# Hybrid attention and RWKV-7 encoder block on one core: two packed transpositions a scan unit instead of four, and rounded products for the head sums, the LoRA's low parts and the attention spreadings

## What is computed

```python
h = rms_norm(x, norm1_w)
z_attn, z_rwkv, z_gate = split(h @ w_in)          # one projection, 12064 columns
q, k = rms_norm(per head of 64) ; o_attn = sum over 3 groups of share * attention(q, k, v)
kk = k_raw * k_k ; kk = kk / sqrt(sum over the head's 64 of kk * kk)
decay = f(decay_w0 + tanh(w_lo) @ decay_w2) ; iclr = sigmoid(iclr_a0 + a_lo @ iclr_a2)
S = S diag(w) + (S (-kk)) (kk*a)^T + v k^T ; y = S r     # per head, forward and backward
x = x + (gates_a * (o_attn @ w_branch_attn) + gates_b * (o_rwkv @ w_branch_rwkv)) @ w_out
x = x + (silu(h2 @ w_gate) * (h2 @ w_up)) @ w_down        # h2 = rms_norm(x, norm2_w)
```

## Time and profile before

| | |
|---|---|
| median of 3 runs | 3433.13 us (3432.88 to 3439.56) |
| the profiled execution, its own time | 3441.14 us |
| its span, first to last instruction | 3439.4 us |
| TensorE busy | 3350.3 us, 97% |
| TensorE's weight loads | 2746.7 us, 80% |
| VectorE busy | 1901.4 us, 55% |
| ScalarE busy | 1233.8 us, 36% |
| GpSimd busy | 1539.0 us, 45% |
| mean granted TensorE clock | 0.991 |
| products L1597 to L1599, projection | 448.0 + 427.2 + 427.4 us |
| products L756 to L758, scan | 189.3 + 170.4 + 170.9 us |
| GpSimd L430 and L433, inversions | 269.8 + 271.0 us |

### The profile page before, as it was taken

How to read it: one execution, slowest core, us unless ns; L and a number is a source line. 1 busy time by engine, 2 the same in 40 slices (tenths; PEclk the granted TensorE clock), 3 DMA queues, 4 the chain that set the end, 5 groups by cost and what they waited for, 6 DMA issues and landing times.

```text
span 3439.4 us, 42457 instructions
## 1 busy us (share of the span) xinstructions
PE 3350.3 (97%) x16199; PEld 2746.7 (80%) x16199; DVE 1901.4 (55%) x2418; ACT 1233.8 (36%) x1963; POOL 1539.0 (45%) x1461
## 2 busy tenths in 40 slices
PE   7999999999998999999899999999999999999998
PEld 6777787777777888888678878888888888888886
DVE  3655465555557877876342022555556456456556
ACT  4433324444234545554343232223233233233232
POOL 4533333333328888888275433322332233223323
PEclk9999999999899999999999999999999999999999
DMA  5444454433354555554543323333332333333323
GB/s 169 133 132 135 123 156 121 120 115 92 87 151 121 126 133 125 129 143 116 191 153 123 123 74 110 92 111 92 104 112 83 117 99 92 110 92 104 111 83 107
DMA packets 666051, 405.08 MB, mean 118 GB/s; under 512 B 193534, under 2 KB 597178, under 8 KB 665338
## 3 DMA queue, kind: packets, MB, share of 16 engines
q1 hardware_dynamic: 665850, 402.38, 40.3%
HBM read 347.05 MB, written 54.53 MB: 117 GB/s over the span
## 4 chain that ended last, share of the span: by engine, by line
PE 49%; DVE 1%; ACT 0%; issue 0%; POOL 0%; DMA 0%; SPq 0%; DVEq 0%; ACTq 0%; POOLq 0%
PE f_bank L2164 9%; PE f_bank L2165 9%; PE f_bank L2166 9%; PE f_bank L2202 4%; PE f_bank L2204 4%; PE f_bank L2203 4%; PE f_bank L2142 2%; PE f_bank L2143 2%; PE f_bank L2144 2%; PE f_bank L2085 1%; PE f_bank L2087 1%; PE f_bank L2086 1%; PE f_bank L2120 0%; DMA orw_plain<-oat 0%; DVE orw_plain L2658 0%
## 5 line engine op out<-in xcount | busy, mean ns | idle before, releaser
L2453 POOL TENSOR_TENSOR w_lo_b<-w_raw_b,w_hi_b 128x1024 fp32r<-128x1024 f32 x176 | 434.1, 2468 | 905.1 <-ACT w_hi_b L2329 903.1
L1285 POOL TENSOR_TENSOR ring_w_rounded<-ring_w_plain,ring_w_hi 128x1024 fp32r<-128x1024 f32 x138 | 333.7, 2419 | 598.9 <-ACT ring_w_hi L1298 598.9
L2164 PE MATMUL f_bank<-act_rounded,w_lo_b 128*128 128x512 f32 x1408 | 549.5, 390 | 1.2 <-DVE act_rounded L2565 1.2
L2165 PE MATMUL f_bank<-act_rounded,w_hi_b 128*128 128x512 f32 x1408 | 548.1, 389 | 0.0
L2166 PE MATMUL f_bank<-act_rounded,w_hi_b 128*128 128x512 f32 x1408 | 548.0, 389 | 0.0
L1597 PE MATMUL slab_ps<-h_hi,ring_w_rounded 128*128 128x512 f32 x1088 | 448.0, 412 | 2.7 <-DVE h_lo L1434 2.4
L1599 PE MATMUL slab_ps<-h_hi,ring_w_hi 128*128 128x512 f32 x1088 | 427.4, 393 | 0.0
L1598 PE MATMUL slab_ps<-h_lo,ring_w_hi 128*128 128x512 f32 x1088 | 427.2, 393 | 0.0
L2329 ACT CAST w_hi_b<-w_raw_b 128x1024 fp32r<-128x1024 f32 x176 | 185.0, 1052 | 448.7 <-DMA w_raw_b<-in_w_ffn_up_dram 202.2
L2164 PEld LDWEIGHTS f_bank<-act_rounded,w_lo_b 128*128 128x128 f32 x1408 | 264.6, 188 | 55.9 <-DVE act_rounded L2565 1.1
L2166 PEld LDWEIGHTS f_bank<-act_rounded,w_hi_b 128*128 128x128 f32 x1408 | 264.6, 188 | 55.3
(11 more groups left out here) (419 smaller groups left out, 6247.5 us busy)
## 6 DMA issues: line engine op xcount, KB each, us to landing
ring_w_plain<-in_w_in_dram SPq DMA_DIRECT2D x190, 512.0 KB, 4.1
w_raw_b<-in_w_ffn_gate_dram SPq DMA_DIRECT2D x88, 512.0 KB, 3.6
w_raw_b<-in_w_ffn_up_dram SPq DMA_DIRECT2D x88, 512.0 KB, 3.6
w_raw_b<-in_w_ffn_down_dram SPq DMA_DIRECT2D x42, 512.0 KB, 4.1
zt<-slab_out SPq DMA_DIRECT2D x65, 256.0 KB, 4.3
...
```

The costliest lines, as they stand in the source:

```text
L1285: pool.tensor_tensor(raw_half(w_lo, h), raw_half(w_raw, h), hi_half(h).bitcast(F32), ALU.subtract).then_inc(lo_ready, 1)
L2164: pe.matmul(o, wl[:, k, :], act_hi[:, kk, :], start=kk == 0, stop=False)
L2165: pe.matmul(o, wh[:, k, :], act_lo[:, kk, :], start=False, stop=False)
L2453: pool.tensor_tensor(low(r), slab_raw(j % 2), high(r).bitcast(F32), ALU.subtract).then_inc(slab_low, 1)
```

## The change

It does four things.
- The scan's `a` and `v` stand side by side in one tile (`av`), as do `b` and `k` (`bk`), 64 columns each: two transpositions of four products take the place of four. Their results lie one above the other; ScalarE copies each head's block to its place (`heads_down`), and v's straight into a `v_t` that GpSimd set to zero before. `b_bd` and `k_bd`, still needed by `ab` and `ak`, are now made by ScalarE (`bd`, the last of its slot) from `bk`. `a_bd` and `v_bd` are gone.
- The head sums are two rounded products. ScalarE makes the squares twice, plain and rounded, and GpSimd the low part, after a half slab's low part. A tile stands after each.
- The low activations of decay and rate have zeros in the other 64 rows, so that both products of a job have 128 rows.
- The spreadings are two rounded products each; VectorE makes high and low part of the shares. Six stand in each of the last two slots, instead of eight and four, and five tiles ahead of the first. Slots without another rule begin with two tiles.

Left out below: the declarations of the new tiles, the counts, and SP's waits with new names.

```diff
@@ scan: orders and shares @@
-PE_SLOT = (("x1", "u"), ("ab", "v"), ("lx", "u"), ("ak", "v"), ("x3", "u"), ("ta", "v"), ("tb", "v"), ("qg", "u"),
-           ("tk", "v"), ("tv", "v"), ("yh", "u"), ("akv", "v"), ("ts", "u"))
-GATE_SHARE = {"ab": 2, "ak": 2, "tb": 3, "tv": 2, "akv": 3, "ts": 4}
+PE_SLOT = (("x1", "u"), ("ab", "v"), ("lx", "u"), ("ak", "v"), ("x3", "u"), ("av", "v"), ("qg", "u"),
+           ("bk", "v"), ("yh", "u"), ("akv", "v"), ("ts", "u"))
+GATE_SHARE = {"ab": 2, "ak": 2, "av": 3, "bk": 3, "akv": 3, "ts": 3}
 DVE_SLOT = (("ab", "v"), ("xadd", "u"), ("ak", "v"), ("decays", "w"), ("qg", "u"), ("operands", "w"), ("state", "u"))
-ACT_SLOT = (("x1", "u"), ("wx", "u"), ("ta", "v"), ("tb", "v"), ("ux", "u"), ("tk", "v"), ("tv", "v"),
-            ("exps", "w"), ("vbd", "w"), ("st", "u"), ("akv", "v"), ("y", "u"))
+ACT_SLOT = (("x1", "u"), ("wx", "u"), ("ux", "u"), ("at", "v"), ("vt", "v"), ("bt", "v"), ("kt", "v"),
+            ("exps", "w"), ("v", "w"), ("st", "u"), ("akv", "v"), ("y", "u"), ("bd", "w"))
@@ phase_scan @@
-for t in (a_bd, b_bd, k_bd, v_bd, ak_bd, w_bd, u_bd, *d_bd):
+for t in (b_bd, k_bd, ak_bd, w_bd, u_bd, *d_bd):
     pool.memset(t[:, :, :], 0.0).then_inc(zeroed, 1)
 for t in low:
+    pool.memset(t[:, :, :], 0.0).then_inc(zeroed, 1)
+for t in v_t:
     pool.memset(t[:, :, :], 0.0).then_inc(zeroed, 1)
 for it in range(NUNIT // 2):
     m = blocks[it % 2]
...
+def heads_down(dst, src):
+    for e in range(2):
+        ins = act.copy(dst[CH * e:CH * e + CH, :, :], src[:, :, CH * e:CH * e + CH])
+    ins.then_inc(taken_act, 1)
@@ phase_scan, ScalarE @@
-elif name == "ta":
-    act.wait_ge(made, PE_AT["ta", n])
-    compact(xar[st][:, :, CH:P], bank[4], taken_act)
-elif name == "tb":
-    act.wait_ge(made, PE_AT["tb", n])
-    compact(rb[st][:, :, CH:P], bank[5], taken_act)
+elif name == "at":
+    act.wait_ge(made, PE_AT["av", n])
+    heads_down(xar[st][:, :, CH:P], bank[4][0:CH, :, :])
+elif name == "vt":
+    if n == 0:
+        act.wait_ge(zeroed, N_ZERO + NSET)
+    for e in range(2):
+        r = slice(CH * e, CH * e + CH)
+        ins = act.copy(v_t[st][r, :, r], bank[4][CH:P, :, r])
+    ins.then_inc(taken_act, 1)
+elif name == "bt":
+    act.wait_ge(made, PE_AT["bk", n])
+    heads_down(rb[st][:, :, CH:P], bank[1][0:CH, :, :])
+elif name == "kt":
+    heads_down(rk[st][:, :, CH:P], bank[1][CH:P, :, :])
...
-elif name == "tk":
-    act.wait_ge(made, PE_AT["tk", n])
-    compact(rk[st][:, :, CH:P], bank[1], taken_act)
-elif name == "tv":
-    act.wait_ge(made, PE_AT["tv", n])
-    act.copy(v_t[st][:, :, :], bank[4][:, :, :]).then_inc(taken_act, 1)
...
-elif name == "vbd":
+elif name == "v":
     act.wait_ge(landed, 96 * (n + 1))
     if n >= 1:
-        act.wait_ge(made, PE_AT["tv", n - 1])
+        act.wait_ge(made, PE_AT["av", n - 1])
+    act.copy(av[:, :, CH:P], ordered(v_in, s)).then_inc(taken_act, 1)
+elif name == "bd":
+    act.wait_ge(taken_dve, DVE_AT["operands", n])
+    if n >= 1:
+        act.wait_ge(made, PE_AT["ak", n - 1])
     for e in range(2):
         r = slice(CH * e, CH * e + CH)
-        ins = act.copy(v_bd[r, :, r], ordered(v_in, s)[r])
+        act.copy(b_bd[r, :, r], bk[r, :, 0:CH])
+    for e in range(2):
+        r = slice(CH * e, CH * e + CH)
+        ins = act.copy(k_bd[r, :, r], bk[r, :, CH:P])
     ins.then_inc(taken_act, 1)
 elif name == "akv":
@@ phase_scan, VectorE @@
 if n >= 1:
-    dve.wait_ge(made, PE_AT["tv", n - 1])
+    dve.wait_ge(made, PE_AT["bk", n - 1])
...
-for e in range(2):
-    r = slice(CH * e, CH * e + CH)
-    dve.tensor_tensor(b_bd[r, :, r], ordered(b0, s)[r], by_scan(e_inv, s)[r], ALU.mult)
-    dve.tensor_tensor(k_bd[r, :, r], ordered(k_in, s)[r], by_scan(e_inv, s)[r], ALU.mult)
+dve.tensor_tensor(bk[:, :, 0:CH], ordered(b0, s), by_scan(e_inv, s), ALU.mult)
+dve.tensor_tensor(bk[:, :, CH:P], ordered(k_in, s), by_scan(e_inv, s), ALU.mult)
 dve.wait_ge(prep_ready, n + 1)
-for e in range(2):
-    r = slice(CH * e, CH * e + CH)
-    ins = dve.tensor_copy(a_bd[r, :, r], t[r, :, CH:P])
-ins.then_inc(taken_dve, 1)
+dve.tensor_copy(av[:, :, 0:CH], t[:, :, CH:P]).then_inc(taken_dve, 1)
@@ phase_scan, TensorE @@
 elif name == "ab":
-    pe.wait_ge(taken_dve, DVE_AT["operands", n])
-    if n >= 1:
-        pe.wait_ge(taken_act, ACT_AT["tk", n - 1])
+    pe.wait_ge(taken_act, ACT_AT["bd", n])
...
-elif name == "ta":
+elif name == "av":
+    pe.wait_ge(taken_act, ACT_AT["v", n])
     if n >= 1:
-        pe.wait_ge(taken_act, ACT_AT["tv", n - 1])
+        pe.wait_ge(taken_act, ACT_AT["vt", n - 1])
     for q in Q:
-        ins = pe.transpose(bank[4][:, q, :], a_bd[:, q, :], g.ident[:, :])
-elif name == "tb":
-    before = [x for x in (n - AHEAD - 1, n - AHEAD - 2) if has_stage("state", x)]
-    if n >= 1:
-        pe.wait_ge(taken_act, ACT_AT["tb", n - 1])
-    if before:
-        pe.wait_ge(taken_dve, DVE_AT["state", before[0]])
-    for q in Q:
-        ins = pe.transpose(bank[5][:, q, :], b_bd[:, q, :], g.ident[:, :])
+        ins = pe.transpose(bank[4][:, q, :], av[:, q, :], g.ident[:, :])
 elif name == "qg":
     pe.wait_ge(taken_act, ACT_AT["wx", n])
     for q in Q:
         ins = pe.matmul(bank[2][:, q, :], w_bd[:, q, :], rb[st][:, q, :], start=True, stop=True)
-elif name == "tk":
+elif name == "bk":
     pe.wait_ge(taken_dve, DVE_AT["ab", n])
     for q in Q:
-        ins = pe.transpose(bank[1][:, q, :], k_bd[:, q, :], g.ident[:, :])
-elif name == "tv":
-    pe.wait_ge(taken_act, max(ACT_AT["ta", n], ACT_AT["vbd", n]))
-    for q in Q:
-        ins = pe.transpose(bank[4][:, q, :], v_bd[:, q, :], g.ident[:, :])
+        ins = pe.transpose(bank[1][:, q, :], bk[:, q, :], g.ident[:, :])
...
 pe.wait_ge(taken_act, ACT_AT["st", n])
-if has_stage("tb", n + AHEAD):
-    pe.wait_ge(taken_act, ACT_AT["tb", n + AHEAD])
-elif n >= 1 and has_stage("state", n - 1):
-    pe.wait_ge(taken_dve, DVE_AT["state", n - 1])
+before = [x for x in (n - 1, n - 2, n - 3) if has_stage("state", x)]
+if before:
+    pe.wait_ge(taken_dve, DVE_AT["state", before[0]])
@@ pro_pe, pro_dve @@
-stages = [("open", s, 4 if s == A0 else 0)]
+stages = [("open", s, {A0: 4, G0 + 3: 5}.get(s, 2))]
 if s - 2 in NORMS:
-    stages.append(("heads", s - 2, 0))
+    stages.append(("heads", s - 2, 1))
...
 if s == G0 + 3:
-    stages += [("spread", n, 2) for n in range(8)]
+    stages += [("spread", n, 2) for n in range(6)]
 if s == G0 + 4:
-    stages += [("spread", n, 2) for n in range(8, N_BC)]
+    stages += [("spread", n, 2) for n in range(6, N_BC)]
...
-    stages += [("weigh", n) for n in range(8)]
+    stages += [("weigh", n) for n in range(6)]
 if s == G0 + 4:
-    stages += [("weigh", n) for n in range(8, N_BC)]
+    stages += [("weigh", n) for n in range(6, N_BC)]
@@ phase_project, GpSimd and ScalarE @@
     pool.wait_ge(hi_ready, h + 1)
     pool.tensor_tensor(raw_half(w_lo, h), raw_half(w_raw, h), hi_half(h).bitcast(F32), ALU.subtract).then_inc(lo_ready, 1)
+    if h % 2 and (h - 5) // 2 in NORMS:
+        pool.wait_ge(taken_act, ACT_DONE["square", (h - 5) // 2])
+        pool.tensor_tensor(sq_r[:, :], sq[:, :], sq_hi[:, :].bitcast(F32), ALU.subtract).then_inc(sq_low, 1)
     if h == 2 * Q0 + 3:
         attention_windows(pool, g, att_consts, dist_abs)
     if h == 2 * Q0 + 5:
     high_h(k)
     if k in (3, 9):
         high(1 + k // 6)
+act.wait_ge(const_ready, 7)
+act.copy(ones_r[:, :], g.head_ones[:, :]).then_inc(sums_ready, 1)
+act.wait_ge(att_consts, 2)
+act.copy(sel_r[:, :], g.sel[:, :, :].rearrange("h a b -> h (a b)")).then_inc(sums_ready, 1)
...
-act.activation(sq[:, :], out_of(n)[:, :], ACT.Square, scale=scale_k).then_inc(taken_act, 1)
+act.activation(sq[:, :], out_of(n)[:, :], ACT.Square, scale=scale_k)
+act.activation(sq_hi[:, :], out_of(n)[:, :], ACT.Square, scale=scale_k).then_inc(taken_act, 1)
@@ phase_project, VectorE @@
-less(x_lo[above, :], lora[above, 0, :], xw_r[above, :])
-ins = less(x_lo[below, :], lora[below, 0, :], xa_r[below, :])
+dve.memset(xw_lo[below, :].bitcast(F32), 0.0)
+dve.memset(xa_lo[above, :].bitcast(F32), 0.0)
+less(xw_lo[above, :], lora[above, 0, :], xw_r[above, :])
+ins = less(xa_lo[below, :], lora[below, 0, :], xa_r[below, :])
...
 link(dve.reciprocal(total, total))
 for gr in range(3):
     ins = dve.tensor_tensor(m_row[gr], m_row[gr], total, ALU.mult)
+link(ins)
+for gr in range(3):
+    ins = dve.tensor_copy(m_hi[gr], m_row[gr])
+link(ins)
+for gr in range(3):
+    ins = dve.tensor_tensor(m_lo[gr], m_row[gr], m_hi[gr].bitcast(F32), ALU.subtract)
 ins.then_inc(taken_dve, 1)
@@ phase_project, TensorE @@
-pe.wait_ge(taken_act, ACT_DONE["square", n])
+pe.wait_ge(sums_ready, 2)
+pe.wait_ge(sq_low, NORMS.index(n) + 1)
 before = norm_before(n)
 if before is not None:
     pe.wait_ge(taken_dve, DVE_DONE["floor", before])
-ins = pe.matmul(heads_ps[:, :], g.head_ones[:, :], sq[:, :], start=True, stop=True)
+pe.matmul(heads_ps[:, :], ones_r[:, :], sq_r[:, :], start=True, stop=False)
```

(10 more changed lines are left out.)

26 lines of the change are left out of this document (16 added, 10 removed).

## The result

| | before | after |
|---|---|---|
| median | 3436.35 us (4 runs, 3432.88 to 3441.06) | 3407.35 us (4 runs, 3404.71 to 3409.48) |
| the profiled execution | 3441.14 us | 3404.71 us (span 3403.0) |
| mean granted clock | 0.991 | 0.989 |

The account below looks back on a forecast made before the run. TensorE was taken to bound the projection, GpSimd's inversions the scan. Head sums 11.5, LoRA 12.8, spreadings 11.7 and scan 10.2 sum to 46.2 us off 3433.13: 3387.0 us, range 3368 to 3402.

Parts of the forecast that it names:

- The sign: Whole kernel: faster than before, chance 0.94; same 0.02, slower 0.04.
- the steady prices: Projection on TensorE: head sum 0.91 us instead of 1.33, LoRA job 0.68 instead of 1.08, spreading interval 2.25.
- rival 3: LoRA products: rows are not what makes the pair dear, 12.8 us less gain, 3399.8 us; chance 0.08.
- 7.5 us of clock: Spreadings: a shorter pair leaves only a short clock dip, giving back 7.5 of 10 us lost.
- the idle becomes 1.7: TensorE's idle before the first spreading grows from 1.12 to 1.7 us, a loss of 0.6.
- The scan's term: Scan: fifteen periods of GpSimd's inversions 0.62 us shorter, the first 0.9 us sooner; 10.2 us, bounds 0 and 28.
- The slope of 0.116: Scan: each microsecond of VectorE lengthens a GpSimd inversion by 0.116 us, so 3.8 less gives 0.44.
- 1 (GpSimd freed wholly): Scan: inversions fall by up to 3.8 us and TensorE leads, full 28 us gained, 3369.2 us; chance 0.13.
- 4 (the scan gives nothing): Scan: GpSimd's inversion length does not move and its pace of 39.21 us stays, 3397.2 us; chance 0.12.
- 5: Scan: ab waits for ScalarE's copies and the kernel is slower, 3463 us at 3 us a slot; chance 0.04.
- 6: Head sums and spreadings: rounded pairs cost what plain ones do, 17.9 us less gain, 3404.9 us; chance 0.02.
- Rival 2: Spreadings: the clock stays low as the idle grows to 1.7 us, 7.5 us come back, 3394.5 us; chance 0.12.

Follow-up runs that it names:

- old_spread: The changed kernel with the spreadings and shares of the kernel before (float32, eight and four, no tiles ahead): 3415.53 us, ratio 0.9934.
- open_rows: The changed kernel with no tiles instead of two before the turned rows: 3406.23 us, ratio 0.9908.
- low_one: The changed kernel with the scan's low gate weights made by a one-input operation (high part times zero), so left out: 3384.8 us, single run.

## Why the prediction was wrong

**The sign and the steady prices held.** The head sums, the LoRA and the interval of the spreadings came to within 0.01 to 0.02 us of each steady price. The 64 rows of the LoRA's first product were what made the pair dear: rival 3 is refuted, 13.9 us against its 0. The Trainium skill's statement (TensorE: Matmul & The Clock Gate, "Why this matters for your kernels") that a product of 32 rows takes the time of one of 128 doesn't hold for a 64-row product between tiles of 128 rows here: 0.40 us extra, gone with the padding.

**The step that failed first is the 7.5 us of clock in "Spreadings".** The forecast took the slow stretch of one profiled execution for a property of the kernel and gave three quarters of it back, because the new pair is shorter. The same instructions ran in 38.5 us at the full clock in other executions. Over the traces the time at half clock there went from 5.5 us (five traces) to 13.7 (eight), so the change lost some 4 us of clock where 7.5 were to come back; that is an estimate from few traces, half of 13.7 less 5.5. The mean clocks of the executions, 0.992 before and 0.987 to 0.989 after, point the same way. What sets the length of such a stretch is open.

That the profiled pair did get something back is luck: (20.5 - 10.2)/2 = 5.1 us. With 0.42 x 12 = 5.0 for the rounding and less 3.9 for the longer wait that is 6.2, what the stage shows.

The base of the forecast was low too: 3433.13 was the median of three, and 70 more executions have 3438.3. How much of the profiled execution's slow stretch was in the median isn't shown: executions with as low a mean clock are common, but where in them it was low is unknown.

**The second is "the idle becomes 1.7".** It became 5.05. The added casts were cheaper than priced (0.41 us). What the forecast left out is where the chain stands: two more tiles at the head of the slot of the turned rows moved it 1.4 us nearer to the start of GpSimd's low parts, and the stretching grew from 2.6 to 6.9 us. old_spread, open_rows and the head sums alone (4.0 us) show it from three sides; the spreadings alone, in the chain's old place, still wait 3.0. The first head sum has the same miss, 3.8 instead of 1.6: GpSimd's 1.2 us became 3.3 beside a subtraction of VectorE. The Trainium skill (SBUF — State Buffer, "Who interferes with whom") calls the shared port an exclusive lock. For these operations of two inputs the traces agree (2.77 for 0.68, 3.33 for 1.3); the forecast weighed it for the scan alone.

**The scan's term** was 15 x 0.62 + 0.9 = 10.2 and came to 7.9 in the profiled pair, to 9.3 in the mean of the seven kernels with the scan of after and the four with that of before. That it came so near is in part luck. The pair fell by 0.41 here and by 0.48 in that mean, 7.2 us in fifteen periods where 9.3 were forecast; the first inversion began 2.9 us sooner instead of 0.9, and the end gave back 0.7. The waits gave 0.32 (forecast 0.18), the length 0.10 to 0.17 (forecast 0.44). The slope of 0.116 was read between a stretch with the gate slabs' subtractions and one without them, where low_one shows 1.3 of the 2.5 us to be theirs; yet short operations added cost 0.13 or more a microsecond. Why those that were removed gave back less than a half of that is open: neither their height, nor their rows, nor ScalarE's copies explain it.

**Rivals.** 1 (GpSimd freed wholly) and 4 (the scan gives nothing) did not come, nor did 5: ab waited for ScalarE once, 0.9 us. 6 is refuted by the 0.90. Rival 2 (the clock stays low) is the nearest, with a longer idle than it reckoned with; its 3394.5 leaves out the two waits. Of the 46.2 us, 9.2 are missing from the sum of terms in the profiled pair (5.5 of them in the two longer waits), and about 7 more stand between that pair and the medians, 4.8 above the one and 2.6 below the other.
